# Moving a column-maximum exchange one page later, and reordering the norm steps in an output-projection loop

## The reference, cut to what matters

```
h = rms_norm(x, norm_mix);  z = h @ w_in            # queries, key/value latent, conv input
for each page of a sequence:                        # attend_sample, 16 pages and the new tokens
    k_nope, v = expand_kv(cache_ckv[page]);  k_nope = rms_norm(k_nope)
    sc = q_nope . k_nope + q_pe . cache_kpe[page]
    m, l, acc = online_update(m, l, acc, sc, v)     # softmax with its maximum
conv = silu(layer_norm(depthwise_conv(glu)))        # width 31
mix = concat(rms_norm(attn), rms_norm(conv))
x = x + mix @ w_out
h = rms_norm(x, norm_ffn)
x = x + (silu(h @ w_gate) * (h @ w_up)) @ w_down
x = x + sigmoid(rms_norm(x) @ w_ple_gate) * (pe @ w_ple_proj)
```

## Time and profile before

| what | value |
|---|---|
| time, median of 3 runs | 1919.13 us (1918.41 to 1925.08) |
| the profiled execution's own time | 1925.08 us |
| its span | 1923.3 us |
| TensorE matmul, busy | 1813.1 us, 94% |
| VectorE, ScalarE, GpSimd busy | 1061.1, 516.2, 374.2 us |
| paged stage and output projection together | about 500 to 980 us after the start |

### The profile page before, as it was taken

How to read it: one execution, slowest core, us unless ns; L and a number is a source line. 1 busy time by engine, 2 the same in 40 slices (tenths; PEclk the granted TensorE clock), 3 DMA queues, 4 the chain that set the end, 5 groups by cost and what they waited for, 6 DMA issues and landing times.

```text
span 1923.3 us, 28150 instructions
## 1 busy us (share of the span) xinstructions
PE 1813.1 (94%) x10492; PEld 1600.7 (83%) x10492; DVE 1061.1 (55%) x1806; ACT 516.2 (27%) x1003; POOL 374.2 (19%) x244
## 2 busy tenths in 40 slices
PE   7999799999899998879999999999999999996998
PEld 7999687778887887768798998998998998995775
DVE  5466886776888788756534334334334334325342
ACT  5212354444443443534321111111111111112110
POOL 2204690001545445423300000000000000003000
PEclk9999899999999999989999999999999999997999
DMA  6310001000411222120030110110120120103011
GB/s 202 99 31 19 7 1 51 2 0 16 129 51 50 60 60 59 50 94 0 3 98 22 55 58 21 52 61 21 49 64 21 46 65 22 44 0 117 28 44 37
DMA packets 109965, 91.79 MB, mean 48 GB/s; under 512 B 25572, under 2 KB 97793, under 8 KB 109870
## 3 DMA queue, kind: packets, MB, share of 16 engines
q1 hardware_dynamic: 107875, 89.63, 15.4%
q10 hardware_dynamic: 2002, 1.03, 0.2%
HBM read 84.73 MB, written 6.26 MB: 47 GB/s over the span
## 4 chain that ended last, share of the span: by engine, by line
PE 77%; DVE 12%; POOL 7%; issue 2%; ACT 1%; DMA 1%; SPq 0%; DVEq 0%; POOLq 0%; ACTq 0%
PE ps L1790 21%; PE ps L1792 20%; PE ps L1791 20%; DVE arena L1302 4%; PE ps L2000 4%; PE ps L1977 3%; POOL arena L809 2%; POOL stats L697 2%; PE ps L2137 2%; PE ps L2251 2%; DVE arena L1643 2%; PE ps L1987 2%; PE ps L473 1%; POOL arena L740 1%; DVE arena L1515 1%
## 5 line engine op out<-in xcount | busy, mean ns | idle before, releaser
L1790 PE MATMUL ps<-h_hi,w_hi 128*128 128x384 f32 (+1 forms) x1056 | 346.2, 328 | 2.9 <-POOL h_lo L804 2.9
L1791 PE MATMUL ps<-h_lo,w_hi 128*128 128x384 f32 (+1 forms) x1056 | 346.1, 328 | 0.0
L1792 PE MATMUL ps<-h_hi,w_lo 128*128 128x384 f32 (+1 forms) x1056 | 346.0, 328 | 0.0
L1737 DVE TENSOR_TENSOR gate_s<-gate_s,ps 128x384 f32<-128x384 f32 (+1 forms) x66 | 35.1, 532 | 339.1 <-PE ps L1792 339.1
L809 POOL TENSOR_TENSOR arena<-arena,mhalf 128x32 f32<-128x32 f32 x32 | 173.8, 5430 | 171.7 <-DVE arena L1664 171.7
L1745 DVE TENSOR_TENSOR arena<-arena,ps 128x512 f32<-128x512 f32 (+1 forms) x198 | 136.0, 687 | 126.3 <-PE ps L1792 126.3
L1790 PEld LDWEIGHTS ps<-h_hi,w_hi 128*128 128x128 f32 x1056 | 199.1, 189 | 4.0 <-issue 3.1
L1791 PEld LDWEIGHTS ps<-h_lo,w_hi 128*128 128x128 f32 x1056 | 199.1, 189 | 0.5
L1792 PEld LDWEIGHTS ps<-h_hi,w_lo 128*128 128x128 f32 x1056 | 199.2, 189 | 0.0
L1790 PE MATMUL ps<-cw_hi,pT_hi 128*128 128x288 f32 x512 | 163.4, 319 | 5.8 <-DVE pT_lo L1562 4.7
L835 POOL TENSOR_TENSOR w_pg_lo<-w_pg,w_pg_hi 128x4096 fp32r<-128x4096 f32 x2 | 17.9, 8944 | 763.5 <-ACT w_pg_hi L1233 763.5
(11 more groups left out here) (285 smaller groups left out, 3570.4 us busy)
## 6 DMA issues: line engine op xcount, KB each, us to landing
arena<-in_cache_ckv SPq DMA_DIRECT2D x128, 128.0 KB, 2.1
w_raw<-in_w_gate SPq DMA_DIRECT2D x22, 512.0 KB, 4.1
w_raw<-in_w_up SPq DMA_DIRECT2D x22, 512.0 KB, 5.3
arena<-in_x_prompt SPq DMA_DIRECT2D x16, 512.0 KB, 5.4
w_uk<-in_w_down SPq DMA_DIRECT2D x11, 512.0 KB, 5.8
w_uv<-in_w_down SPq DMA_DIRECT2D x11, 512.0 KB, 5.9
gw_raw<-in_w_in SPq DMA_DIRECT2D x8, 512.0 KB, 6.2
w_out<-in_w_out SPq DMA_DIRECT2D x1, 4096.0 KB, 13.6
```

The lines of the kernel that those rows point to most:

```text
L1790: mm(out, left[0], right[0], start=start, stop=False)
L1791: mm(out, left[0], right[1], start=False, stop=False)
L1792: return mm(out, left[1], right[0], start=False, stop=stop)
```

## The change

In the paged stage seven steps of the softmax chain move one page later on their engine: `max_T` from g = 4 to 5, `max_B` 5 to 6, `pv` 8 to 9 on TensorE; `row_of_max` 4 to 5, `shift` 5 to 6, `out_lat` 11 to 12 on VectorE; `soft_exp` 7 to 8 on ScalarE. `last_quad` and `lat_T` stay.

In the output projection's loop three lists are put in another order. VectorE's `residual` comes before `variance` and `layer_norm`, and `mix_scale` becomes the last step; ScalarE does `high_m(j, 1)` and `x2_square(j - 1)` before `conv_silu(j + 1)`; GpSimd does `nt_pool` between `ln_pool` and `mix_pool`. No instruction is added or taken away.

```diff
@@ GpSimd
                 if j + 1 < NT:
                     ln_pool(j + 2, rows_of(OUT_TILES[j + 1]))
+                nt_pool(pool, "c", j, P, 0)
+                if j + 1 < NT:
                     mix_pool(j + 2, rows_of(OUT_TILES[j + 1]))
-                nt_pool(pool, "c", j, P, 0)
@@ ScalarE
-                    if g == 7 and b >= 1:
+                    if g == 8 and b >= 1:
                         soft_exp(b - 1, 1 - s)
...
                     centred_square(j + 1)
-                    conv_silu(j + 1)
                 high_m(j, 1)
                 x2_square(j - 1)
-                if j + 1 == NT:
+                if j + 1 < NT:
+                    conv_silu(j + 1)
+                else:
                     act.wait_ge(s_("gu_loaded0"), 32)
@@ VectorE
-                    if prev and g == 4:
+                    if prev and g == 5:
                         row_of_max(b - 1, 1 - s)
...
-                    if prev and g == 5:
+                    if prev and g == 6:
                         shift(b - 1, 1 - s)
-                    if prev and g == 11:
+                    if prev and g == 12:
                         out_lat(b - 1, 1 - s)
...
                     centre(j + 1)
-                    variance(j + 1)
-                    layer_norm(j + 1)
                 residual(j - 1)
                 if j < NT:
                     low_m(j, 1)
                 if j + 1 < NT:
-                    mix_stat(j + 1)
+                    variance(j + 1)
                 nt_dve_mean(dve, "c", j, rows_of(OUT_TILES[j - 1]), 0)
+                if j + 1 < NT:
+                    layer_norm(j + 1)
                 if j >= 2:
                     gain_h(j - 2)
                 if j + 1 < NT:
+                    mix_stat(j + 1)
+                nt_dve_scale(dve, "c", j, x2[0:rows_of(OUT_TILES[j - 1]), OUT_TILES[j - 1], :], rows_of(OUT_TILES[j - 1]), 0, xn2)
+                if j + 1 < NT:
                     mix_scale(j + 1)
-                nt_dve_scale(dve, "c", j, x2[0:rows_of(OUT_TILES[j - 1]), OUT_TILES[j - 1], :], rows_of(OUT_TILES[j - 1]), 0, xn2)
@@ TensorE
-                    if b and g == 4:
+                    if b and g == 5:
                         max_T(b - 1)
-                    if b and g == 5:
+                    if b and g == 6:
                         max_B(b - 1)
-                    if b and g == 8:
+                    if b and g == 9:
                         pv(b - 1, 1 - s)
```

## The result

The changed kernel takes 1951.25 us (median of 4 runs, 1947.7 to 1953.16) against 1918.87 us: the ratio is 1.016, with a 95% interval of 1.0134 to 1.0184. I had forecast 1921 us and a range up to 1930. The kernel became about 31 us slower, and the time lies outside the range. The slowest rival that I had priced, a lower clock behind each pause of the projection, stood at 1932 us.

A forecast was written before the change was run, and what follows sets the result against it. TensorE's pace was taken to set the time almost everywhere (77% of the chain). Paged stage -7 and projection +9 gave +2 us: 1921 us against the median of 1919.13, range 1909 to 1930.

The forecast's parts named there:

- a lower clock behind each pause of the projection: Rival: each `m_T` pause in the output projection lowers the clock; projection +20, paged stage -7, 1932 us; chance 0.12.
- The paged stage, forecast -7 us: Softmax chain one page later: -1.0 us in each of six sequences, -1 us at `chunk_T` before sequence 7.
- forecast 2.7: Paged stage: new `pair_T` wait for page loads, 2.7 us in six sequences, with a clock drop of 1.62 us each.
- forecast 10.95: Paged stage: earliest start of `pair_T` after `pv` ends, 0.75 us plus 10.2 us for the loads.
- forecast 19.2: Paged stage: TensorE's time after `pv`: 10.95 us to `pair_T`, 6.6 for three pages, 1.6 for the clock.
- VectorE's 17.0: Paged stage: VectorE's time from the end of `pv` to `quad` after the change, 17.0 us against 19.0 before.
- the fall of the clock at `max_T`: Paged stage: low clock after the 1.74 us wait, priced at 1.62 us; wait and clock together -3.36 us a sequence.
- The projection, forecast +9 us: Output projection: the longer chain starts `m_T` 7.5 instead of 6.21 us after `residual`, 1.3 us late in seven iterations.
- `mix_scale`, two steps of 0.48 that overlap a little, 0.87: Output projection: last step of the chain before `m_T`, 0.87 us plus a release of 0.1, ending at 7.5 us.
- no clock loss at 1.3 us: Output projection: the 1.3 us `m_T` pause, below the 1.54 us that kept the clock at 1.00, adds no clock cost.
- The bound that I gave for the projection, 0 to +20: Output projection: 0 if overlaps are larger than read; 7 x (1.3 + 1.62) = +20 if every pause drops the clock.
- The point between 1.54 and 1.74 us: Clock-loss rival for the projection: the pause length, between the nearest rows of either kind, beyond which the clock drops.

The follow-up runs named there:

- the paged half alone: The kernel before with only the seven steps of the softmax chain one page later, projection lists unchanged: 1910.91 us, ratio 0.9967.
- the kernel with `pv` left in place: Kernel before with only `max_T`, `row_of_max`, `max_B` and `shift` one page later; `soft_exp`, `pv`, `out_lat` unmoved: 1924.32 us, ratio 1.0013.

## Why the prediction was wrong

**The paged stage, forecast -7 us, measured -6.3.** Its mechanism held. The waits of `max_T` and the low clock behind them went. `pair_T` waits 2.3 to 3.1 us, forecast 2.7, and starts 10.5 to 10.9 us after `pv` in the paged half alone, forecast 10.95. The clock falls at six of six of these waits in the changed kernel and at four of six in the paged half alone. `chunk_T` before sequence 7 waits 4.0 us instead of 5.1, forecast 1 us less. `kpe_T` comes 18.3 to 18.6 us after `pv` in four sequences of the paged half alone, forecast 19.2. Removing the bound of the loads brought out VectorE's 17.0 at 16.9. That the two totals lie so close is in part luck. The stretch behind `pv` was taken 0.6 to 0.9 us too long in each sequence, and the fall of the clock at `max_T` was credited six times, where five other executions with the old order at this place show it four or five times of six.

**The projection, forecast +9 us, measured +38.** This is the step that failed: "`mix_scale`, two steps of 0.48 that overlap a little, 0.87". They took 2.95 us (905.85 to 908.80). The duration was read from a row in which GpSimd was idle, and the reordering moves the step on top of `low_h`; I had `gain_h` down as hidden, left `high_h` and `low_h` out of the working, and did not ask what runs at the new place. Two terms of the sum were mis-sized by it: the first step of `mix_scale`, 0.48 in the sum and 2.56 us measured, and GpSimd's power, 0.71 and 1.13 us. In iterations 2 to 7 they bring the wait from 1.1 to 3.6 us. The second effect follows from the first: I took no clock loss at 1.3 us, and behind the six waits of 1.01 to 1.14 us there was none; but at 3.6 us the clock falls each time. For iteration 1 my own numbers disagreed: its wait of 1.54 us stood in the rows already, so 1.3 more makes 2.8, beyond the 1.74 that I took for a fall. It measured 2.81 us with a fall. The experiments divide the loss: the longer chain +10.6 us (forecast +9), the power beside `nt_dve_scale` about 5, the collision of `mix_scale` with `low_h` about 22. Of these 22, six times 2.07 us are waiting, 12.4 us. The rest, some 10 us, is put down to the clock: with the collision it falls at all seven waits, without it at two. No run has the long waits without the falls, so this share is a remainder and was not measured alone.

**The rivals.** That the projection lowers the clock had 0.12 and was the right direction for the wrong reason: its price of +20 took the pause at 1.3 us. No rival had two engines in each other's way. The bound that I gave for the projection, 0 to +20, was made from the rows of operations running alone, and so it was no bound. The point between 1.54 and 1.74 us at which a pause was to lower the clock does not exist as such: a pause of 1.45 us lowered it, and pauses of 1.73 and 2.01 us did not each time.

**What stays open.** The timed gain of the paged half (6.3 us) is smaller than its profiles show (8.5 us). The falls of the clock, at 1.62 us each, explain most of the 4 us between profiles of the same code (317.9 with six falls at `max_T`, 313.7 with four); how many falls a timed run has was not measured. Nor did any run show why the clock falls at one wait and not at another of the same length.

## What to carry to other kernels

When an operation is moved, its duration must be read again for its new neighbours: list what the other engines run at that time, and for VectorE above all what GpSimd runs. A chain with a slack of 1 us that feeds TensorE is worth guarding, because here pauses of 1.5 to 1.57 us left the clock alone in the reordered loop, and pauses of 3.6 us lowered it for 3.5 to 7 us each time. And a wait that shows in the list costs nothing while another engine binds the same stretch; find which one comes last before paying for its removal.

## What the runs showed of the hardware

- A `tensor_scalar` of 128x512 on VectorE took 2.56 us beside a GpSimd subtraction of 128x1024 that had started 0.07 us before it, and 0.485 us otherwise; as `tensor_tensor` 2.82 and 0.69 us. It ended 0.30 us after GpSimd did, so most of its 0.485 us came then: it looks held, and not merely slowed.
- The other way round, GpSimd's small power of two columns took 1.13 us when it met a 0.75 us `tensor_scalar` of 128x1024, and 0.70 us otherwise. The power of one column (`nt_pool`, L467) took 1.02 us beside `layer_norm` and 0.55 in the kernel before; it was not on the path.
- GpSimd's power of 128x32 ran 5.43 us and left a VectorE instruction with two SBUF operands inside it at its 1.27 us.
- Whether the clock falls behind a pause was not settled by its length between 1.4 and 2.4 us. The pause of 1.72 to 1.74 us at `max_T` lowered it 27 times in the 36 cases of six executions with the old order at this place. In the kernel with `pv` left in place six pauses of 2.01 us were followed by a low clock three times and by 1.00 three times; in the paged half alone a pause of 2.38 us was followed by 0.57 and one of 2.29 us by 1.00:

```profile
587.50:591.50 4.00, 4.00 (x21) 4.00 (x21) 3.69 (x6) 1.21 (x3) 1.91 (x1) 0.57 0.48 131
671.50:675.50 4.00, 3.99 (x31) 3.99 (x32) 3.85 (x9) 1.31 (x3) 2.81 (x1) 1.00 0.41 131
```
